# Moving the tables buffer to a multiple of 128 bytes in a two-block network with routed experts

## The reference

```python
D_MODEL = 1024
N_EXPERTS = 8
TOP_K = 2
D_EXPERT = 7 * D_MODEL // 2        # 3584

def swiglu(t, w_gate, w_up, w_down):
    return (jax.nn.silu(t @ w_gate) * (t @ w_up)) @ w_down
```

## Time and profile before

| | us |
|---|---|
| median of 3 runs | 2878.68 |
| lowest and highest | 2874.83 and 2879.66 |
| the profiled execution, time | 2879.11 |
| the profiled execution, span from first to last instruction | 2877.3 |

### The profile page before, as it was taken

One profiled execution on the slowest core, in us unless ns is written; L12 is line 12 of the kernel. 1 busy time (PEld: TensorE's weight loads), 2 busy tenths in 40 slices (PEclk: granted clock), 3 DMA queues, 4 the chain that ended last, 5 costly groups with the idle time before them and its releaser, 6 DMA issues.

```text
span 2877.3 us, 38890 instructions
## 1 busy us (share of the span) xinstructions
PE 2695.6 (94%) x15420; PEld 2268.4 (79%) x15420; DVE 1818.0 (63%) x1905; ACT 1464.0 (51%) x1626; POOL 29.5 (1%) x40
## 2 busy tenths in 40 slices
PE   6999889999898899889899998899999999999998
PEld 3875568888796799777789986788888888888886
DVE  3224565553544676573355454588888888888886
ACT  3226333332335454532144444477777777777775
POOL 0001000000002000000000000000000000000000
PEclk8999999999998999996899999899999999999999
DMA  7446413222231444320035441599999999999996
GB/s 301 181 178 258 164 59 117 88 103 81 103 125 39 173 167 171 127 88 1 1 118 189 170 160 60 188 363 342 364 344 341 358 342 363 343 365 345 339 367 226
DMA packets 84359, 590.43 MB, mean 205 GB/s; under 512 B 9616, under 2 KB 10000, under 8 KB 19472
## 3 DMA queue, kind: packets, MB, share of 16 engines
q1 hardware_dynamic: 82800, 576.79, 53.9%
q10 hardware_dynamic: 1440, 11.93, 1.1%
HBM read 587.63 MB, written 1.05 MB: 205 GB/s over the span
## 4 chain that ended last, share of the span: by engine, by line
PE 84%; DVE 8%; ACT 4%; issue 2%; DMA 1%; DVEq 0%; POOL 0%; ACTq 0%; SPq 0%; POOLq 0%
PE banks L469 23%; PE banks L470 22%; PE banks L471 22%; PE banks L475 15%; DVE ring_rounded L531 2%; ACT ring_rounded L521 1%; DMA ring<-in_stream 1%; PE banks L2794 1%; PE banks L844 1%; DVE rstd L756 1%; DVE scratch L716 0%; DVE aT L769 0%; DVE aT L2192 0%; DVE hT L1518 0%; DVE activations L1356 0%
## 5 line engine op out<-in xcount | busy, mean ns | idle before, releaser
L531 DVE TENSOR_TENSOR ring_rounded<-ring,ring_rounded 128x2048 fp32r<-128x2048 f32 (+4 forms) x168 | 339.6, 2023 | 452.2 <-ACT ring_rounded L521 451.2
L470 PE MATMUL banks<-aT_rounded,ring_rounded 128*128 128x256 f32 (+1 forms) x1632 | 530.8, 325 | 0.0
L470 PE MATMUL banks<-ring_rounded,activations_rounded 128*128 128x512 f32 x1344 | 527.5, 392 | 0.0
L521 ACT ACTIVATE ring_rounded<-ring 128x2048 fp32r<-128x2048 f32 (+4 forms) x168 | 284.6, 1696 | 397.6 <-PE banks L471 388.8
L469 PE MATMUL banks<-aT_rounded,ring_rounded 128*128 128x256 f32 (+2 forms) x1120 | 338.3, 302 | 23.3 <-DVE aT_rounded L778 11.6
L470 PEld LDWEIGHTS banks<-aT_rounded,ring_rounded 128*128 128x128 f32 x1632 | 317.0, 194 | 23.9 <-issue 0.7
L471 PE MATMUL banks<-aT_rounded,ring_rounded 128*128 128x256 f32 (+2 forms) x1120 | 335.4, 299 | 0.0
L470 PEld LDWEIGHTS banks<-ring_rounded,activations_rounded 128*128 128x128 f32 x1344 | 252.7, 188 | 52.3
L2968 DVE TENSOR_TENSOR ring_rounded<-ring,tables_rounded 128x2048 fp32r<-128x2048 f32 x112 | 253.6, 2288 | 28.6 <-ACT tables_rounded L2886 28.5
L2886 ACT ACTIVATE tables_rounded<-ring 128x2048 fp32r<-128x2048 f32 x112 | 215.0, 1920 | 95.5 <-DMA ring<-in_stream 89.6
L2968 DVE TENSOR_TENSOR ring_rounded<-ring,aT_rounded 128x2048 fp32r<-128x2048 f32 x112 | 254.0, 2286 | 12.2 <-ACT aT_rounded L2886 12.1
(11 more groups left out here) (317 smaller groups left out, 4802.9 us busy)
## 6 DMA issues: line engine op xcount, KB each, us to landing
ring<-in_stream SPq DMA_DIRECT2D x501, 1024.0 KB, 5.3
ring<-in_stream SPq DMA_DIRECT2D x32, 704.0 KB, 5.5
ring<-in_stream SPq DMA_DIRECT2D x28, 768.0 KB, 6.0
activations<-in_rpb ACTq DMA_DIRECT2D x2, 1536.0 KB, 7.1
ring<-in_stream SPq DMA_DIRECT2D x6, 512.0 KB, 5.1
tables<-in_tab_b ACTq DMA_DIRECT2D x1, 2436.0 KB, 8.8
tables<-in_tab_a ACTq DMA_DIRECT2D x1, 2304.0 KB, 8.7
hT<-in_h ACTq DMA_DIRECT2D x1, 2048.0 KB, 15.6
```

The source lines that it names most:

```text
L470: pe.matmul(out, exact(upper), exact(w_lower), start=False, stop=False)
L521: act.activation(exact(upper), w, ACT.Copy).then_inc(g.s["act_pieces"], 1)
L531: dve.tensor_tensor(exact(w), w, rounded(upper), ALU.subtract).then_inc(g.s["dve_pieces"], 1)
```

## The change

The buffer vectors is entered behind scratch instead of ahead of tables, so that tables begins at 114816, a multiple of 128. The table `mod_rows` gets 32 columns instead of 16 and `expert_no` 32 instead of 8; where `expert_no` is read, the first eight columns are taken. With that every table begins at a multiple of 128 bytes too. The tables' buffer has 5792 elements instead of 5776. hT, aT and ring stay where they were, tables lies 2496 bytes lower, and mod_rows through scratch lie 2432 bytes lower. No instruction, wait or order changes.

```diff
--- before.py
+++ after.py
@@ -59,7 +59,7 @@
     out["ident"] = np.eye(P)
     out["ones"] = np.ones((P, P))
     out["mean"] = np.full((P, P), 1.0 / D)
-    out["mod_rows"] = (p[:, None] % 32 == np.arange(16)[None, :]) * 1.0
+    out["mod_rows"] = (p[:, None] % 32 == np.arange(32)[None, :]) * 1.0
     out["headones"] = (p[:, None] // HD == p[None, :] // HD) * 1.0
 
     c = p % HD
@@ -103,7 +103,7 @@
     out["mean"] = np.full((P, P), 1.0 / D)
     out["before"] = (p[:, None] < p[None, :]) * 1.0
     out["slot_no"] = np.broadcast_to(np.arange(128.0), (P, P))
-    out["expert_no"] = np.broadcast_to(np.arange(8.0), (P, 8))
+    out["expert_no"] = np.broadcast_to(np.arange(32.0), (P, 32))
     out["headones"] = (p[:, None] // HD == p[None, :] // HD) * 1.0
     out["causal"] = np.where(p[None, :] <= p[:, None], 0.0, NEG)
     same = p[:, None] // CH == p[None, :] // CH
@@ -2696,10 +2696,10 @@
         g.count("dve_routing")
         dve.wait_ge(sem, g.so_far("dve_routing"))
         for n, a in ((0, 40), (1, 48)):
-            dve.tensor_scalar(f(t, a, 8), g.tab("expert_no"), f(t, 24 + n, 1), f(t, 35 + n, 1), ALU.is_equal,
+            dve.tensor_scalar(f(t, a, 8), g.tab("expert_no")[:, 0:8], f(t, 24 + n, 1), f(t, 35 + n, 1), ALU.is_equal,
                               ALU.mult).then_inc(sem, 1)
             g.count("dve_routing")
-            dve.tensor_scalar(f(t, a + 16, 8), g.tab("expert_no"), f(t, 24 + n, 1), None, ALU.is_equal).then_inc(sem, 1)
+            dve.tensor_scalar(f(t, a + 16, 8), g.tab("expert_no")[:, 0:8], f(t, 24 + n, 1), None, ALU.is_equal).then_inc(sem, 1)
             g.count("dve_routing")
         dve.wait_ge(sem, g.so_far("dve_routing"))
         dve.tensor_tensor(g.rt[:, 0:NE, 2 + t], f(t, 40, 8), f(t, 48, 8), ALU.add).then_inc(sem, 1)
@@ -3316,7 +3316,6 @@
         g.ring = g.sb_both("ring", RING + 1, SLOT)
 
         g.piece_upper = [g.ring[:, RING, SLOT // 2 * i:SLOT // 2 * i + SLOT // 2] for i in range(2)]
-        g.vec = g.sb("vectors", nv)
         na, nb = io["tab_a"].shape[1], io["tab_b"].shape[1]
         g.tabs = g.sb_both("tables", max(na + 2 * 384, nb))
         g.tab_at = packed(tables_a())[1]
@@ -3328,6 +3327,7 @@
         g.nmax, g.rsum, g.rinv = g.sb("nmax", 2, 2), g.sb("rsum", 2, 2), g.sb("rinv", 2, 2)
         big = g.sb_both("activations", 14976)
         tmp = g.sb_both("scratch", 4608)
+        g.vec = g.sb("vectors", nv)
         g.big, g.tmp = big, tmp
 
         def part(t, at_, *shape):
```

## The result

The change made the kernel slower. The median of 11 runs is 2890.4 us (2881.2 to 2894.3), against 2878.3 us (2872.1 to 2882.1, 11 runs) for the kernel before; the ratio is 1.0039, with a 95% interval of 1.0027 to 1.0051. The forecast was 2867.2 us, in a range of 2864 to 2875.

The account below looks back on a forecast made before the run. TensorE was taken to bound the expert stage. The profiled 2879.1 us less 11.5 for tables, the other parts taken as nothing, gave 2867.6, and 2867.2 us against the runs' median; range 2864 to 2875.

Parts of the forecast that it names:

- What bounds the kernel: Expert stage, 1849 to 2860 us: TensorE busy 1003.9 of 1011 us, so a matmul's cost there is paid in full.
- Part (1): Expert stage: tables at a multiple of 128 brings slow units to 2.72 us, 1.44 us per expert, 11.5 us for eight.
- DMA estimate: Expert stage: with 11.5 us less, DMA must move 351 GB/s, which fits with 5% to spare.
- three neighbors that served as witnesses: Expert units in aT, ring and scratch, buffers beginning at multiples of 128: 2.72 us against 2.80 to 2.82 with tables.
- Part (5): All else moves down: mod_rows through scratch 2432 bytes lower, tables 2496; hT, aT and ring stay; taken as 0.
- Rival (c): Slower: cost hangs on the moving and stationary pair, 14 ns per read; worst case 18.8 us, giving 2886.0 us; chance 0.05.
- Rival (b): The tables units' cost belongs to something else that tables keeps, so the time stays 2878.7 us; chance 0.12.
- 16-byte rule: Skill's lines of 16 bytes: tables 64 bytes off is on a boundary already, so nothing would be won, 2878.7 us.
- Parts (2), (3) and (4): ScalarE and VectorE on tables 0; plain fp32 matmuls reading tables 0, 3 us allowed; padding 0.02 and 0.03 us per load.

Follow-up runs that it names:

- experiment 1: The kernel before with vectors and tables exchanged in place, no padding, all other buffers where they were; 2868.4 us, ratio 0.9967.
- experiment 5: Network left out, TensorE alone: 512-column fp32r matmuls at all pairs of operand starts in 32-byte steps; 227 to 228 ns level, 229 to 234 otherwise.
- experiment 7: experiment 5 with 4-byte steps, shorter operands and plain fp32; 512 columns from 4 to 252 bytes 228.4 to 239.8 ns, plain fp32 215.8 ns a record.
- experiment 10: The changed kernel with activations 128 bytes further on and scratch at 208256, vectors behind scratch and padding kept; 2867.4 us, ratio 0.9969.
- experiment 4: experiment 1 with hT, aT, ring, tables, vectors and mod_rows through activations 128 bytes further on, scratch staying; 2875.8 us, ratio 0.9987.
- experiment 9: experiment 8 with level blocks before and after each other pair; 512 columns level 227 ns, 5.26 us for 23 gaps right behind a slow block.
- experiment 8: experiment 5 in the order of `mm3`, two moving operands taking turns at separate distances; 229 to 234 ns in the six 512-column blocks shown.

## Why the prediction was wrong

**What bounds the kernel** was right: TensorE paces the expert stage, and the stage became shorter in experiment 1 and longer in the changed kernel by what its units gained and lost.

**Part (1), the tables,** was right in size and reach when done alone: 11.5 us counted, (125.50 - 124.09) x 8 = 11.3 measured in the stage by experiment 1 and 9.0 between the medians; its 2868.4 us is near the 2867.2 forecast. The DMA estimate held too: the stage of experiment 1 moves 351 GB/s, the number worked out. What was wrong is the reason. The tables units were not slow because tables begins off a multiple of 128, but because it isn't level with activations, where the stationary operands lie. The three neighbors that served as witnesses for "a multiple of 128 is fast" were all level with activations, and that went unseen.

**Part (5) is the step that failed.** "All else moves down: I take 0." It was put at nothing without a look at what it moves against what: activations and scratch went down by 19 x 128 bytes, an odd number of halves of 256, against ring and aT. Against the kernel before, whose tables units were slow already, that cost 6.7 us in the experts. Ahead of them, product by product in the two traces, those of 512 columns that read activations or scratch with ring take 5.5 us more (6 ns for 372 and 244 products of L469, 7 ns for 176 of L470, 1 to 2 ns for those of L471), those of 384 columns 0.8 us more, those of 256 columns with activations 1.4 us less, and those of aT with ring, between and behind the others, 1.3 us less: 3.7 us in all. That is 10.4 of the 12.1 us between the medians; for the rest no run shows a cause. Against experiment 1, which has the gain alone, the medians differ by 2890.4 - 2868.4 = 22.0 us, of which the experts hold (126.34 - 124.09) x 8 = 18.0 and the rounded products ahead of them 3.4.

**Rival (c) is what happened,** and it had a chance of 0.05. Its mechanism was right: the pair and not the address. Its price was 14 ns per read; in the changed kernel, where all twelve reads of a unit are off level, it is (2.79 - 2.72) / 12 = 6 ns. Its worst case took 18.8 us from the experts, and 18.0 is what they lost, but by luck: more than twice the right price, on a third of the reads (the 1344 of L470, where all 4032 are off level). The measured time lies 4 us above its 2886.0, and what it left out is the first block. The argument that held it down failed: "activations is paired with ring, aT and scratch at quite different distances, and all those units are at 2.72." The distances are 397, 461 and 234 times 256. Different as numbers, they are one and the same modulo 256, and the addresses to see it stood in the text ahead of the prediction.

**Rival (b) and the 16-byte rule.** Experiment 1 answers (b): in another place the same tables units take 2.72 us. In "SBUF — State Buffer", section "Specifications (TRN2)", the Trainium skill gives lines of 16 bytes, by which a start 64 or 128 bytes on would change nothing. The runs differ: 24 matmuls take 5.47 us level and 5.60 us at a distance of 128 bytes, in the grid of TensorE alone (experiment 5), and the measurement decides.

**Parts (2), (3) and (4)** held. In the changed kernel the subtraction of VectorE takes 2286 ns with tables and 2283 with scratch, against 2288 and 2285. The transposes of L2794, whose identity is now at a multiple of 128, take 272 ns as before, and plain fp32 takes 215.8 ns a record at all eight starts of experiment 7. With the padding kept in experiment 10 nothing was left over.

**Still open:** why the period is 256 bytes; why 64 ahead is nearly as good as level if all reads are so and not if four of twelve are level, while with 128 ahead it is the other way round; 1.7 us of the changed kernel and some 3 us of experiment 4; and whether 256-column products could be given the 2 ns that a distance other than 0 saves: a buffer would have to be level in one stage and not in another, and it wasn't tried.

## What to carry to other kernels

Before a buffer is moved, write down the start of every pair that TensorE reads together, as moving minus stationary, modulo 256, before and after. For rounded products of 512 columns keep it at 0; for those of 256 columns that is not the best. A witness that something doesn't matter must differ in the quantity that the rival names; distances that look different may be equal modulo the period. Where the layout is tight, exchange two buffers so that all others keep their places, as in experiment 1, rather than shift everything behind one.

## What the runs showed of the hardware

For fp32r products of 512 columns on TensorE alone, all reads at one distance, the pace from start to start is 227 to 228 ns with level operands, 229 at 64 bytes and 232 to 234 ns at all other multiples of 32 bytes, with period 256 bytes (experiment 5). After a slow block it took nine matmuls to come back (experiment 9). Neither side's own alignment matters: both moved together by 32 bytes take the same 228 ns (5.47 us for 24). Some starts between the steps of 32 bytes reach 240 ns (experiment 7). Where two moving operands at different distances take turns, the pair decides: 229 ns for (128, 0) and (192, 128), 233.5 and 234 for (64, 0) and (192, 0) (experiment 8). For 256 columns the sign is turned, 120 ns level and 118 off (experiment 9). For plain fp32 of 256 columns there is no effect, 215.8 ns a record at eight starts (experiment 7).
